# Second LayerNorm of blocks 0 to 3: sums turned in 32x32 blocks on VectorE, rows stored in 128-byte runs

## The chip, the cores and the metric

The kernel runs on one core of one Trainium2 chip. The metric is the device time of one execution in microseconds (us); the median of three runs is given. Of the core's engines, TensorE multiplies matrices and, through a product with the identity, turns them; VectorE and ScalarE work on tiles; GpSimd has small jobs here; SyncE only issues transfers. A transfer is issued by an engine's instruction and done by 16 DMA engines beside it.

## The reference

One layer of a hybrid decoder: a projection, four token mixers, an output projection, then an MLP with squared ReLU, each followed by a LayerNorm on the scaled residual. Only the last line matters here.

```python
def layer_norm(x, g, b):
    xf = x.astype(jnp.float32)
    mu = jnp.mean(xf, -1, keepdims=True)
    var = jnp.mean(jnp.square(xf - mu), -1, keepdims=True)
    return ((xf - mu) * lax.rsqrt(var + LN_EPS) * g + b).astype(x.dtype)
...
x = layer_norm(ALPHA * x + mix, ln1_g[l], ln1_b[l])
x = layer_norm(ALPHA * x + sq_relu_mlp(x, w_ff1[l], w_ff2[l]), ln2_g[l], ln2_b[l])
```

2080 tokens (2048 of a prompt, 32 of eight decoded sequences) of 1024 channels are computed in fp32. The MLP has 4096 hidden channels.

## The kernel before

The tokens are cut into 5 blocks of 416 (BLK). Activations lie channels first: a tile is 128 channels x 416 tokens, 8 tiles (KT) are a block's 1024 channels. Every fp32 product is made of three of rounded values: each weight tile (128 x 1024, 512 KB) and each activation is split into a high part (ScalarE, L1391 for weights) and the rest (VectorE, L1917), and TensorE does high x high, high x low and low x high (L1106 to L1108) for the 8 channel tiles: 24 matmuls of 416 columns.

After the input projections and the first part of the attention the program is one long list of steps n, one weight tile each. A block has 72 steps (STEPS_B); base_of(b) is its first, and r counts from there. Its steps are "up" and "down" tiles of the MLP in turns (0 to 7 up, 8 to 15 down, and so on), then the next block's output projection. Each engine's program walks through the same steps and does at each what is due:

- SyncE, at step n, requests weight tile n + 4 (load_weights, L650). It waits until VectorE has split tile n + 2, since two raw tiles have a place (w_raw). Behind that, in this order, come transfers of an attention unit (load_q L667, load_k L677, load_v L704), the gather of one K page in four transfers (gather_k, L774) and stores of finished rows (store_row, L756). It runs its program strictly in order.
- ScalarE, at step n, finishes the activation of tile n - 1 if that is an up tile (hidden), then splits tile n + 2 (hi_ahead), once step n - 1 is done (three split tiles have a place), then makes the two sigmoids of the attention unit of this step (L1360, L1364).
- VectorE, at step n, adds the result of tile n - 1 or makes the low part of its activation (hidden_lo, L1944), in block 3 does sample work, splits tile n + 2 (lo_ahead), then does its part of the attention, then of a LayerNorm.
- TensorE, at step n, starts with the scores of the step's attention unit (L950, L951). They wait for ScalarE's sigmoids of the unit before, since the scores have a single PSUM bank. In every fourth such step it multiplies the attention output (L965). Then come the 24 matmuls.

Attention units stand in steps 8 to 53, 8 to 59 and 8 to 53 of blocks 0, 1 and 2. The gathers stand in two of three steps until step 47 of block 2. Block 3 has the attention of the decoded sequences instead: from step K_AT = 10 on VectorE turns two K pages (turn_pages, L2154) at each step, ahead of its split of the weights. SyncE loads the first four at step 9 (L524).

The second LayerNorm of block b - 1 is done in steps 1, 2, 4 and 6 of block b (ROWS2), a group of 104 rows at each. TensorE turns the sums (acc, "mlp_sum") of the group into rows, with 8 transposes into two PSUM banks (forward, L1139). VectorE takes mean and variance of each row from there (bn_stats, L1958; bn_aggr), ScalarE the root (L1428), VectorE scales and adds (L2127, L2129) into nat3, and SyncE stores the group one step later. nat3 shares its place with other tiles (pages of the samples, y_block, the first LayerNorm's work tiles), so load_y and the first K pages of block 3 wait for the stores (s_out). Block 4's rows are done after the last step, and this the change leaves alone.

## Time and profile before

| | us |
|---|---|
| median of three runs | 2357.74 (2355.44 to 2365.38) |
| the profiled execution | 2362.01 |
| its span, first to last instruction | 2360.3 |
| TensorE busy with matmuls | 2308.6 |
| VectorE busy | 1534.7 |
| ScalarE busy | 1143.7 |
| GpSimd busy | 211.0 |

TensorE's granted clock was 0.995 of full over the span. Busy time is a union: neighbours that overlap are counted once. In a listing by group the mean is that of one instruction from its start to its end, so that a mean may be above the pace at which such instructions follow each other. The DMA engines were busy 48.7% of their time for SyncE's queue. Splitting a weight tile takes ScalarE 1.05 us and VectorE 1.22, the low part of an activation 0.59. Issuing the store of a row group keeps SyncE for 0.42 us in the median (0.40 to 0.51), and the next request follows 0.55 us after its start (956.27 to 956.82 in block 1).

### The profile page before, as it was taken

Reading aid. Unit: us, or ns where it says so; the run is one execution under the profiler, and the core shown is the slowest. Engines: PE = TensorE matmul, PEld = TensorE weight load, DVE = VectorE, ACT = ScalarE, POOL = GpSimd, SP = SyncE. Lnnn points to the kernel's source line nnn. Section 1 sums busy time; section 2 is a strip of 40 time slices with the busy share of each in tenths; the row PEclk is TensorE's granted clock in tenths of the full one; section 3 lists DMA queues with packets and bytes.
Section 4 is the critical chain, followed back from the end, with each engine's and each line's share of the span. In section 5 each row is a group of like instructions: output and inputs, shape, how many; then the busy total and the mean of one; then the engine's idle time right before and its main releaser. Section 6 shows DMA issues by size and latency. Waiting matters only on the chain.

```text
span 2360.3 us, 45447 instructions
## 1 busy us (share of the span) xinstructions
PE 2308.6 (98%) x17231; PEld 2217.8 (94%) x17231; DVE 1534.7 (65%) x2175; ACT 1143.7 (48%) x1740; POOL 211.0 (9%) x464
## 2 busy tenths in 40 slices
PE   7999999999999999999999999999999999999998
PEld 6999999899989999999999999999988889999997
DVE  7545661845777778777778778767876426854435
ACT  5466522545546545465464555544534425444432
POOL 0012230200111100100110011100000320000000
PEclk9999999999999999999999999999999999999999
DMA  8434553644665544665654556543377774343332
GB/s 260 147 111 141 164 176 133 190 134 126 164 194 171 157 143 132 170 189 145 187 154 135 159 150 189 164 133 126 119 280 239 252 233 146 107 146 116 117 115 83
DMA packets 219180, 377.38 MB, mean 160 GB/s; under 512 B 105409, under 2 KB 140738, under 8 KB 218834
## 3 DMA queue, kind: packets, MB, share of 16 engines
q1 hardware_dynamic: 209682, 346.45, 48.7%
q0 software_dynamic: 9280, 28.02, 3.7%
q8 instruction: 137, 2.24, 0.4%
q14 instruction: 81, 0.66, 0.1%
HBM read 327.37 MB, written 63.80 MB: 166 GB/s over the span
## 4 chain that ended last, share of the span: by engine, by line
PE 91%; DVE 2%; ACT 2%; DMA 2%; issue 1%; SPq 1%; DVEq 0%; ACTq 0%
PE PS L1106 22%; PE PS L1108 22%; PE PS L1107 21%; PE PS L890 5%; PE PS L892 5%; PE PS L891 5%; PE PS L965 3%; PE PS L951 1%; PE PS L950 1%; DMA w_raw<-w_all 1%; PE PS L1030 1%; PE PS L1005 1%; PE PS L930 1%; PE PS L1139 1%; DVE w_hi_lo L1917 1%
## 5 line engine op out<-in xcount | busy, mean ns | idle before, releaser
L1391 ACT ACTIVATE w_hi_lo<-w_raw 128x1024 fp32r<-128x1024 f32 x240 | 252.9, 1054 | 366.7 <-PE PS L1108 292.9
L1106 PE MATMUL PS<-a_hi,w_hi_lo 128*128 128x416 f32 x1080 | 383.3, 355 | 2.8 <-issue 1.6
L1108 PE MATMUL PS<-a_hi,w_hi_lo 128*128 128x416 f32 x1080 | 379.3, 351 | 0.8 <-issue 0.8
L1107 PE MATMUL PS<-a_lo,w_hi_lo 128*128 128x416 f32 x1080 | 378.5, 350 | 0.0
L1917 DVE TENSOR_TENSOR w_hi_lo<-w_raw,w_hi_lo 128x1024 fp32r<-128x1024 f32 x240 | 292.5, 1219 | 79.0 <-ACT w_hi_lo L1391 77.2
L1106 PE MATMUL PS<-h_hi,w_hi_lo 128*128 128x416 f32 x824 | 291.1, 353 | 0.0
L1108 PE MATMUL PS<-h_hi,w_hi_lo 128*128 128x416 f32 x824 | 289.3, 351 | 0.0
L1107 PE MATMUL PS<-h_lo,w_hi_lo 128*128 128x416 f32 x824 | 288.2, 350 | 0.4 <-issue 0.4
L1944 DVE TENSOR_TENSOR h_lo<-h_full,h_hi 128x416 fp32r<-128x416 f32 x160 | 94.5, 591 | 249.2 <-ACT h_hi L1406 249.0
L1106 PEld LDWEIGHTS PS<-a_hi,w_hi_lo 128*128 128x128 f32 x1080 | 203.1, 188 | 11.7 <-issue 7.5
L1402 ACT ACTIVATE h_full<-PS 128x416 f32<-128x416 f32 x160 | 82.3, 514 | 261.4 <-PE PS L1108 255.2
L1107 PEld LDWEIGHTS PS<-a_lo,w_hi_lo 128*128 128x128 f32 x1080 | 203.4, 188 | 4.8 <-issue 1.7
L1391 ACT ACTIVATE w_hi_lo_c<-w_raw 128x1024 fp32r<-128x1024 f32 x120 | 126.4, 1053 | 167.9 <-PE PS L1108 154.9
L1108 PEld LDWEIGHTS PS<-a_hi,w_hi_lo 128*128 128x128 f32 x1080 | 202.7, 188 | 2.3
L1106 PE MATMUL PS<-a_hi,w_hi_lo_c 128*128 128x416 f32 x520 | 185.1, 356 | 3.5 <-DVE a_lo L1950 3.3
L1108 PE MATMUL PS<-a_hi,w_hi_lo_c 128*128 128x416 f32 x520 | 183.9, 354 | 0.0
L1107 PE MATMUL PS<-a_lo,w_hi_lo_c 128*128 128x416 f32 x520 | 183.1, 352 | 0.0
L1872 DVE TENSOR_TENSOR_SCAN n_prompt<-n_prompt 128x512 f32<-128x512 f32 (+3 forms) x160 | 177.4, 1109 | 4.6 <-POOL n_prompt L2389 3.9
L1917 DVE TENSOR_TENSOR w_hi_lo_c<-w_raw,w_hi_lo_c 128x1024 fp32r<-128x1024 f32 x120 | 146.3, 1219 | 38.6 <-ACT w_hi_lo_c L1391 37.4
L1106 PEld LDWEIGHTS PS<-h_hi,w_hi_lo 128*128 128x128 f32 x824 | 154.6, 188 | 7.4 <-issue 4.7
L1107 PEld LDWEIGHTS PS<-h_lo,w_hi_lo 128*128 128x128 f32 x824 | 154.9, 188 | 3.2
L1937 DVE TENSOR_TENSOR mlp_sum<-mlp_sum,PS 128x416 f32<-128x416 f32 x117 | 68.6, 587 | 135.6 <-PE PS L1108 134.4
(313 smaller groups left out, 4708.3 us busy)
## 6 DMA issues: line engine op xcount, KB each, us to landing
...
k_gathered<-ck SPq DMA_DIRECT2D x512, 32.0 KB
...
proj_scratch<-stage SPq DMA_DIRECT2D x70, 208.0 KB, 2.0
...
```

The costliest lines, as they stand in the source:

```text
L890: pe.matmul(out, w_h, x_hi(b)[:, k, :], start=(k == 0), stop=False)
L891: pe.matmul(out, w_h, x_lo(b)[:, k, :], start=False, stop=False)
L892: ins = pe.matmul(out, w_l, x_hi(b)[:, k, :], start=False, stop=(k == KT - 1))
L965: ins = pe.matmul(PS[HD * side:HD * side + HD, 3 + quarter, first * 32:P], vq[rows, k + side, :], wt[rows, v % 2, first:4, k + side, :], s ...
L1106: pe.matmul(out, w_h, mh_[:, k, :], start=(g == 0), stop=False)
L1107: pe.matmul(out, w_h, ml_[:, k, :], start=False, stop=False)
L1108: ins = pe.matmul(out, w_l, mh_[:, k, :], start=False, stop=(g == KT - 1))
L1391: act.activation(halves(w_hi(n)), raw_halves(n), ACT.Copy).then_inc(s_wh, 1)
L1402: act.activation(hf[:, f % 2, :], PS[:, (N_P + n) % 3, 0:BLK], ACT.Relu).then_inc(s_r, 1)
L1872: dve.tensor_tensor_scan(rev(n_t[:, 0:w]), rev(n_t[:, 0:w]), rev(n_t[:, 0:w]), n_t[:, w:w + 1], ALU.mult, ALU.bypass).then_inc(s_scan2, 1)
L1917: dve.tensor_tensor(halves(w_lo(n)), raw_halves(n), halves(w_hi(n)).bitcast(F32), ALU.subtract).then_inc(s_wl, 1)
L1944: dve.tensor_tensor(hl[:, i, :], hf[:, f % 2, :], hh[:, i, :].bitcast(F32), ALU.subtract).then_inc(s_hl, 1)
```

## The change

For blocks 0 to 3 nothing is turned on TensorE any more. VectorE's transpose turns each 32x32 block of a tile for itself. Applied to acc[:, k, :], 128 channels x 416 tokens, it gives a tile in which partition 32 q + j, at place (i, 32 k + c), holds token 32 i + j and channel 128 k + 32 q + c. So each group of 32 partitions, a quadrant, holds for every token a quarter of its channels. Mean and variance of those 256 values are taken, and joined over the four quadrants with two small products with a matrix gmean, which holds 0.25 where partition numbers agree modulo 32: one for the mean, one for the variance within plus the squared deviation of the quadrant's mean. The gains and shifts are loaded a second time in the quadrants' order (gq). A row of the output is then four times eight runs of 32 values, and the store of one channel tile and one quadrant is a transfer of 32 partitions x 13 runs of 128 bytes; a block has 32 of them.

The work is placed in steps 0 to 7 of the next block, the stores in steps 8 and 9 behind everything else that SyncE issues in those steps. The sample attention of block 3 starts two steps later (K_AT = 12, V_AT = 35), and its first K pages are loaded in step 11. TensorE waits at step 8 for the variance instead of the rows.

```diff
-ROWS2 = (1, 2, 4, 6)
+TB = BLK // 32
+PART = ((0, 7), (7, TB))
+SCALED_AT = (6, 7)
+STORED = 16 * 4 * KT
+MEAN_AT = {base_of(b) + r: (b - 1, which) for b in range(1, NB) for which, r in enumerate((4, 5))}
...
-K_AT, V_AT = 10, 33
+K_AT, V_AT = 12, 35
...
-            def store_row(b, j):
-
-                sp.wait_ge(s_row, b * NR + j + 1)
-                sp.dma_start(y_out[b * BLK + j * ROW:b * BLK + (j + 1) * ROW], nat3[0:ROW, j, :]).then_inc(s_out, 16)
+            def store_rows(b, ks):
+
+                rows = y_out[b * BLK:(b + 1) * BLK].rearrange("(i j) (k r c) -> k r j i c", j=32, r=4, c=32)
+                sp.wait_ge(s_row, b + 1)
+                for k in ks:
+                    for q in range(4):
+                        sp.dma_start(rows[k, q], nat4[32 * q:32 * q + 32, :, 32 * k:32 * k + 32]).then_inc(s_out, 16)
...
             sp.dma_start(gb2[:, :, :], rows2).then_inc(s_gb, 16)
+            for q in range(4):
+                rows = rows2[32 * q:32 * q + 32].rearrange("p n (k r c) -> p n k r c", r=4, c=32)[:, :, :, q, :]
+                sp.dma_start(gq[32 * q:32 * q + 32, :, :].rearrange("p n (k c) -> p n k c", c=32), rows).then_inc(s_gb, 16)
...
-                    if r == 9:
-                        sp.wait_ge(s_out, 16 * NR * 3)
+                    if r == 11:
+                        sp.wait_ge(s_out, STORED * 3)
                         for u in range(RING):
                             k_load(sp, u)
...
-                if b >= 1 and r - 1 in ROWS2:
-                    store_row(b - 1, ROWS2.index(r - 1))
+                if b >= 1 and r in (8, 9):
+                    store_rows(b - 1, range(4 * r - 32, 4 * r - 28))
...
-            def norm2_row(b, j):
-
-                if j == 0:
-                    pe.wait_ge(s_fev, (b + 1) * FT)
-                if j >= 2:
-                    pe.wait_ge(s_row, b * NR + j - 1)
-                forward(acc, 0, j, 0)
+            def norm2_stat(b, which):
+
+                if b == 0 and which == 0:
+                    pe.wait_ge(s_gmean, 1)
+                pe.wait_ge(s_qst, 2 * b + which + 1)
+                src = qsq[:, :] if which else qmv[:, :, 0]
+                pe.matmul(PS[:, 4 + which, 0:TB], gmean[:, :], src, start=True, stop=True).then_inc(s_qsum, 1)
...
+            def norm2_turn(b, ks):
+
+                wait_apart(dve, s_fev, (b + 1) * FT)
+                for k in ks:
+                    own.up(dve.transpose(nat4[:, :, 32 * k:32 * k + 32], acc[:, k, :]))
+
+            def norm2_spread(first, last):
+
+                for i in range(first, last):
+                    own.up(dve.bn_stats(qbn[:, i, :], nat4[:, i, :]))
+
+            def norm2_gain(first, last):
+
+                for i in range(first, last):
+                    own.up(dve.scalar_tensor_tensor(out=nat4[:, i, :], in0=nat4[:, i, :], scalar=qmean[:, i:i + 1], in1=gq[:, 0, :],
+                                                    op0=ALU.subtract, op1=ALU.mult))
+
+            def norm2_rows(b, part):
+
+                for i in range(*PART[part]):
+                    ins = dve.scalar_tensor_tensor(out=nat4[:, i, :], in0=nat4[:, i, :], scalar=qrstd[:, i:i + 1], in1=gq[:, 1, :],
+                                                   op0=ALU.mult, op1=ALU.add)
+                if part:
+                    ins.then_inc(s_row, 1)
+                else:
+                    own.up(ins)
+
+            def norm2(b, r):
+
+                if r == 0:
+                    norm2_turn(b, range(4))
+                if r == 1:
+                    norm2_turn(b, range(4, KT))
+                    own.sync()
+                    norm2_spread(0, 4)
+                if r == 2:
+                    norm2_spread(4, TB)
+                    own.sync()
+                    for i in range(TB):
+                        ins = dve.bn_aggr(qmv[:, i, :], qbn[:, i, :])
+                    ins.then_inc(s_qst, 1)
+                if r == 4:
+                    dve.wait_ge(s_qst, 2 * b + 1)
+                    dve.wait_ge(s_qsum, 2 * b + 1)
+                    own.up(dve.tensor_tensor(qdev[:, :], qmv[:, :, 0], PS[:, 4, 0:TB], ALU.subtract))
+                    op(dve.tensor_copy(qmean[:, :], PS[:, 4, 0:TB]))
+                    op(dve.tensor_tensor(qsq[:, :], qdev[:, :], qdev[:, :], ALU.mult))
+                    dve.tensor_tensor(qsq[:, :], qsq[:, :], qmv[:, :, 1], ALU.add).then_inc(s_qst, 1)
+                    if b == 0:
+                        dve.wait_ge(s_gb, 80)
+                    norm2_gain(0, 5)
+                if r == 5:
+                    dve.wait_ge(s_qsum, 2 * b + 2)
+                    dve.tensor_scalar(qstd[:, :], PS[:, 5, 0:TB], EPS, None, ALU.add).then_inc(s_qve, 1)
+                    norm2_gain(5, TB)
+                if r == 6:
+                    dve.wait_ge(s_qsd, b + 1)
+                    op(dve.reciprocal(qrstd[:, :], qstd[:, :]))
+                if r in SCALED_AT:
+                    norm2_rows(b, SCALED_AT.index(r))
```

SyncE in steps 8 to 10 of block 1, from the request of tile 12 on; y_out is the output, "nat" is nat3, "rows_turned" is nat4. Before:

```order
L650 DMA w_raw<-w_all 128x1024 [waits w_lo_made]
L667 DMA q_rows<-proj_scratch 64x512 [waits q_lo_made]
...
L774 DMA k_gathered<-ck 128x1x64
L650 DMA w_raw<-w_all 128x1024 [waits w_lo_made]
L704 DMA v_quarters<-v_scratch 32x1024 [waits av_done,v_tile_stored]
L704 DMA v_quarters<-v_scratch 32x1024 x3
L677 DMA k_rows<-kv_out 64x512 [waits k_lo_made]
L677 DMA k_rows<-kv_out 64x512
L650 DMA w_raw<-w_all 128x1024 [waits w_lo_made]
```

and with the change:

```order
L667 DMA w_raw<-w_all 128x1024 [waits w_lo_made]
L684 DMA q_rows<-proj_scratch 64x512 [waits q_lo_made]
...
L794 DMA k_gathered<-ck 128x1x64
L776 DMA y_out<-rows_turned 32x13x32 [waits row_scaled]
L776 DMA y_out<-rows_turned 32x13x32 x15
L667 DMA w_raw<-w_all 128x1024 [waits w_lo_made]
L721 DMA v_quarters<-v_scratch 32x1024 [waits av_done,v_tile_stored]
L721 DMA v_quarters<-v_scratch 32x1024 x3
L694 DMA k_rows<-kv_out 64x512 [waits k_lo_made]
L694 DMA k_rows<-kv_out 64x512
L776 DMA y_out<-rows_turned 32x13x32 [waits row_scaled]
L776 DMA y_out<-rows_turned 32x13x32 x15
L667 DMA w_raw<-w_all 128x1024 [waits w_lo_made]
```

Sixteen stores now stand between the requests of tiles 12 and 13, and sixteen more between those of tiles 13 and 14.

SyncE in steps 1 to 10 of block 4, where only weights and rows are moved. Before:

```order
L650 DMA w_raw<-w_all 128x1024 [waits w_lo_made] x20
L756 DMA y_out<-nat 104x1024 [waits row_scaled]
L650 DMA w_raw<-w_all 128x1024 [waits w_lo_made]
L756 DMA y_out<-nat 104x1024 [waits row_scaled]
L650 DMA w_raw<-w_all 128x1024 [waits w_lo_made] x2
L756 DMA y_out<-nat 104x1024 [waits row_scaled]
```

and with the change:

```order
L667 DMA w_raw<-w_all 128x1024 [waits w_lo_made] x26
L776 DMA y_out<-rows_turned 32x13x32 [waits row_scaled]
L776 DMA y_out<-rows_turned 32x13x32 x15
L667 DMA w_raw<-w_all 128x1024 [waits w_lo_made]
L776 DMA y_out<-rows_turned 32x13x32 [waits row_scaled]
L776 DMA y_out<-rows_turned 32x13x32 x15
```

The four single stores, a step or two apart, have become two rows of sixteen with one weight request between them.

VectorE in steps 0 to 2 of block 1 with the change; before, each of steps 1, 2, 4 and 6 held two statistics, a join, the small ones and two scalings of 104x1024:

```order
L2126 STREAM_TRANSPOSE rows_turned<-mlp_sum 128x13x32 [waits mlp_evacuated]
L2126 STREAM_TRANSPOSE rows_turned<-mlp_sum 128x13x32 x3
L1953 TENSOR_TENSOR h_lo<-h_full,h_hi 128x416 [waits h_hi_made]
L1928 TENSOR_TENSOR w_hi_lo<-w_raw,w_hi_lo 128x2x512 [waits w_hi_made]
L2126 STREAM_TRANSPOSE rows_turned<-mlp_sum 128x13x32 [waits mlp_evacuated]
L2126 STREAM_TRANSPOSE rows_turned<-mlp_sum 128x13x32 x3
L2131 BN_STATS quadrant_bn<-rows_turned 128x6 [waits dve_own]
L2131 BN_STATS quadrant_bn<-rows_turned 128x6 x3
L1953 TENSOR_TENSOR h_lo<-h_full,h_hi 128x416 [waits h_hi_made]
L1928 TENSOR_TENSOR w_hi_lo<-w_raw,w_hi_lo 128x2x512 [waits w_hi_made]
L2131 BN_STATS quadrant_bn<-rows_turned 128x6 x9
L2161 BN_AGGR quadrant_mean_var<-quadrant_bn 128x2 [waits dve_own]
```

Everything down to the 13 joins stands ahead of TensorE's first small product, which is in the middle of step 4.

## Rows read from the trace of the kernel before

**Rows 1.** The page: busy time of the engines, and the last chain by engine.
```profile
PE 2308.6 (98%) x17231; PEld 2217.8 (94%) x17231; DVE 1534.7 (65%) x2175; ACT 1143.7 (48%) x1740; POOL 211.0 (9%) x464
PE 91%; DVE 2%; ACT 2%; DMA 2%; issue 1%; SPq 1%; DVEq 0%; ACTq 0%
```
**Rows 2.** Waits of TensorE: who waited for whom, us in total, times, longest.
```profile
PE PS L1106 <- DVE a_lo L1950: 3.3, 4, 1.6
```
**Rows 3.** The chain in block 1's step 1: start, length, what.
```profile
915.71 0.87 PE PS L1139 x8
```
**Rows 4.** TensorE's timeline in step 50 of block 3: start, length, engine, line, operation.
```profile
1949.22 0.35 PE L1108 MATMUL PS<-a_hi,w_hi_lo_c 128*128 128x416 f32 x1
1949.41 0.53 PE L1042 MATMUL PS<-row_pairs,y_rows 128*128 128x32 f32 x4
...
1950.05 0.35 PE L1107 MATMUL PS<-a_lo,w_hi_lo_c 128*128 128x416 f32 x1
```
**Rows 5.** VectorE's timeline in block 1, and groups by form (busy, mean ns of one).
```profile
919.68 1.29 DVE L1958 BATCH_NORM_STATS2 bn<-PS 104x6 f32<-104x512 f32 x2
...
924.66 0.58 DVE L1944 TENSOR_TENSOR h_lo<-h_full,h_hi 128x416 fp32r<-128x416 f32 x1
...
L1887 DVE STREAM_TRANSPOSE w_turned<-s_prompt 128x384 f32<-128x384 f32 x16 | 9.1, 572 | 0.0
...
L2035 DVE SCALAR_TENSOR_TENSOR nat<-nat,rstd,gb 104x512 f32<-104x512 f32 x8 | 5.6, 747 | 0.2
```
**Rows 6.** SyncE: two lines' instructions, a timeline row, and the page's transfers with landings.
```profile
L695 SPq DMA_DIRECT2D v_scratch<-v_made x32: 594/628/1286, 414.0 to 1209.4; - x32
...
L764 SPq DMA_DIRECT2D q_sample<-proj_scratch x4: 427/428/432, 1680.1 to 1682.9; - x4
...
1207.34 2.66 SPq L695 DMA_DIRECT2D v_scratch<-v_made  x4
...
v_scratch<-v_made SPq DMA_DIRECT2D x32, 64.0 KB, 3.4
...
proj_scratch<-stage SPq DMA_DIRECT2D x70, 208.0 KB, 2.0
```
**Rows 7.** SyncE's timeline in steps 8 to 10 of block 1.
```profile
960.66 3.22 SPq L774 DMA_DIRECT2D k_gathered<-ck  x4
963.93 0.47 SPq L650 DMA_DIRECT2D w_raw<-w_all  x1
...
967.54 0.58 SPq L650 DMA_DIRECT2D w_raw<-w_all  x1
```
**Rows 8.** ScalarE's timeline in block 1; TensorE's scores at step 13 of blocks 1 and 2.
```profile
968.46 1.06 ACT L1391 ACTIVATE w_hi_lo<-w_raw 128x1024 fp32r<-128x1024 f32 x1 [3.26 <-DMA w_raw<-w_all]
...
970.56 0.63 ACT L1342 ACTIVATE q_hi_lo<-q_rows 128x512 fp32r<-128x512 f32 x1
...
979.98 0.39 PE L950 MATMUL PS<-k_hi_lo,q_hi_lo 128*128 128x512 f32 x1
...
1368.65 0.39 PE L950 MATMUL PS<-k_hi_lo,q_hi_lo 128*128 128x512 f32 x1
```
**Rows 9.** SyncE's timeline in block 2, then in block 3 with VectorE's two page turns.
```profile
1350.93 0.48 SPq L650 DMA_DIRECT2D w_raw<-w_all  x1
...
1721.26 0.33 SPq L650 DMA_DIRECT2D w_raw<-w_all  x1
1724.82 1.75 SPq L524 DMA_DIRECT2D pages<-k_gathered  x4
...
1728.93 2.50 DVE L2154 STREAM_TRANSPOSE k_pages_turned<-pages 128x1024 f32<-128x1024 f32 x2 [1.30 <-DMA pages<-k_gathered]
```
**Rows 10.** Block 4: a tile request of SyncE, ScalarE's splits at steps 10 and 11.
```profile
2093.01 45.64 SPq L650 DMA_DIRECT2D w_raw<-w_all  x11
...
2098.03 1.06 ACT L1391 ACTIVATE w_hi_lo<-w_raw 128x1024 fp32r<-128x1024 f32 x1 [3.03 <-PE PS L1108]
2102.56 1.06 ACT L1391 ACTIVATE w_hi_lo<-w_raw 128x1024 fp32r<-128x1024 f32 x1 [3.47 <-PE PS L1108]
```

More of the change, by code:

```diff
@@ L838, in _ @@
                         load_x1(b + 1)
-                    if r == (40 if b < 3 else 50):
+                    if r == (40 if b < 3 else 51):
                         load_y(b + 1)
@@ L1097, in dense @@
                         norm1_stat(*STAT_AT[n])
+                    if n in MEAN_AT and g == 4:
+                        norm2_stat(*MEAN_AT[n])
                     if i == 0:
@@ L2009, in last_rows @@
             def last_rows(js, between):
-                e = NR * NB
+                e = NR
                 two = slice(js[0], js[1] + 1)
@@ L2116, in norm1_back, with quadrant_mean @@
                     dve.tensor_tensor(al[:, k, :], xr[:, k, :], ah[:, k, :].bitcast(F32), ALU.subtract).then_inc(s_xl, 1)
-            def norm2_row(b, j):
-                e = NR * (b + 1) + j
-                row_var(e)
-                row_rstd(e)
-                bank = 4 + 2 * (j % 2)
-                row = nat3[0:ROW, j, :]
-                if b == 0 and j == 0:
-                    dve.wait_ge(s_gb, 16)
-                op(dve.scalar_tensor_tensor(out=row, in0=PS[0:ROW, bank:bank + 2, :].rearrange("p a b -> p (a b)"),
-                                            scalar=mv[0:ROW, j, 0:1], in1=gb2[0:ROW, 0, :], op0=ALU.subtract, op1=ALU.mult))
-                dve.scalar_tensor_tensor(out=row, in0=row, scalar=rstd[0:ROW, j:j + 1], in1=gb2[0:ROW, 1, :], op0=ALU.mult,
-                                         op1=ALU.add).then_inc(s_row, 1)
+            def quadrant_mean():
+                m = gmean[:, 0:32]
+                op(dve.tensor_tensor(m, ident[:, 0:32], ident[:, 32:64], ALU.add))
+                for q in (2, 3):
+                    op(dve.tensor_tensor(m, m, ident[:, 32 * q:32 * q + 32], ALU.add))
+                op(dve.tensor_scalar(m, m, 0.25, None, ALU.mult))
+                for q in (1, 2, 3):
+                    own.up(dve.tensor_copy(gmean[:, 32 * q:32 * q + 32], m))
+                own.sync()
+                dve.sem_inc(s_gmean, 1)
```

71 lines of the change are left out of this document (31 added, 40 removed).

## Prediction

> **What bounds the kernel now.** I read the page's busy times and its chain first: TensorE is busy for 98% of the span, and 91% of the chain that ended last is its matmuls [rows 1]. Next come TensorE's waits: behind the input projections the largest is 3.3 us in all [rows 2]. So TensorE's instruction stream sets the time, an instruction taken out of it pays in full, and another engine costs nothing until TensorE waits for it. The question is therefore how much each edit removes from that stream, and which other engine comes near enough to hold it up.
>
> A weight tile costs 24 matmuls, one step of 4.53 us where nothing else is in it; rows on ScalarE 4.53 us apart show that [rows 10]. In steps with an attention unit it is 5 us, and about 7.2 where the attention output is multiplied too. I call step r the r-th of a block and count blocks from 0. SyncE runs through the same steps; in step r it requests the tile of step r + 4 as soon as VectorE has split that of r + 2. ScalarE splits tile r + 4 in step r + 2. A late request thus has up to two steps before ScalarE wants it and two more before TensorE does. In blocks 1 and 2 the second pair doesn't count: ScalarE makes the sigmoids of an attention unit behind its split of the weights, and TensorE's next scores wait for them.
>
> **Taken from TensorE.** The second LayerNorm of a block turned its four row groups with 8 transposes each, 128 in four blocks; on the chain one group is 0.87 us [rows 3]. 16 x 0.87 = 13.9 us go. All of it is on the bounding engine.
>
> **Added to TensorE.** Two fp32 products per block, 128x13. The nearest rows are two fp32 products with 32 columns: they put 0.83 us between the matmul before them and the second behind them, where 0.38 is usual [rows 4]. That is 0.45 for two, 1.8 us for four blocks. Cost of PE edits: -13.9 + 1.8 = -12.1 us.
>
> **VectorE.** Before, a row group took from 919.68 to 924.66, 5.0 us, four times a block [rows 5]. Now come 8 transposes of 416 columns at about 0.60 (384 columns take 0.57), 13 statistics of 256 values at somewhat over half the 0.65 of 512, say 0.36, 13 joins of them at an estimated 0.2, and 26 scalings of 256 values at half the 0.75 of 512 values plus 0.1 [rows 5]: 4.8 + 4.7 + 2.6 + 12.4 and 1 us of small ones, 25.5 against 20 us. It is spread over steps 0 to 7, where 8 x 1.65 us of other work (the lower halves of weights and activations) leave 23 of 36 us; what doesn't fit runs some 2 us into step 8, before the stores of the rows can start anyway. So it is hidden. The nearest call is TensorE's first product in the middle of step 4: it wants the 13 joined statistics. From 919.68 on, where its first statistics stand now, VectorE has 2.4 + 1.4 + 1.65 + 3.2 + 2.6 = 11.3 us to do and ends at 931.0; TensorE would come to it at about 915.7 + 3.5 x 4.53 = 931.6 [rows 3, 5]. Hidden by a hair; if statistics of 256 cost the full 0.65 each, it is late by 3 to 4 us in each block. I take 0, and 0 to 16 us for the range. ScalarE's four roots become one: off the path.
>
> **SyncE's queue: the term that decides.** A block's rows were stored in 4 requests of 0.42 us, one in steps 2, 3, 5 and 7. Now they take 32 requests, 16 in step 8 and 16 in step 9, each 32 partitions x 13 runs of 128 bytes. The queue's own instructions take time on SyncE. The nearest row is the store of the turned V tile: 32 partitions x 16 runs of 128 bytes, median 0.63 us, and four of them in 2.66 [rows 6]. I take 0.66 each: 10.6 us for 16, in steps of 4.5 to 5 us. The request for tile 13 stands behind 16 of them, that for tile 14 behind 32. The lower bound for one is the 0.47 at which requests with 2 such runs follow each other, the upper the 0.80 of the page gathers (4 in 3.22) [rows 6, 7]. The data keeps up with that as far as a row tells: such a store lands after 3.4 us, 1.4 more than one with long runs [rows 6].
>
> Block by block, in the clock of the trace of before (removed transposes shift everything alike):
> - Block 1. Tile 13 was requested at 963.93 and ScalarE started on it at 968.46, tile 14 at 967.54 [rows 7, 8]. 0.55 us of the old store goes, 10.6 comes: tile 13 at 974.0. 3.6 us of V and K requests follow, then 10.6 more: tile 14 at 988.2. It lands 4.5 later (as tile 13 did), 992.7, and the sigmoids behind its split are done 2.1 later, 994.8 (968.46 to 970.56 in the rows). TensorE's scores of step 13 stood at 979.98 [rows 8]. **14.8 us lost.**
> - Block 2, with the same steps. 1350.93 - 0.55 + 10.6 = 1361.0; + 3.6 + 10.6 = 1375.2; + 4.5 + 2.1 = 1381.8 against 1368.65 [rows 8, 9]. **13.1 us.**
> - Block 3 has no attention and no gathers, but SyncE waits in step 11 for all stores of block 2 before it loads K pages into their place, and VectorE turns two pages before it splits tile 14. Tile 12 is requested at 1721.26; the last store is issued at 1742.7 and lands 3.4 later, 1746.0; pages take 4.1 (1724.82 to 1728.93), two turns 2.5 and the split 1.2: 1753.8. TensorE ends step 8 some 0.5 us behind the request of tile 12 (in block 4: 2098.03 - 4.53 against 2093.01), at 1721.8, and would start tile 14 five steps and some 0.9 us of sample work later, at 1745.3 [rows 9, 10]. **8.5 us.**
> - Block 4. Tile 12 at 2093.0, tile 14 at 2114.9, landed 4.5 later, split on both engines after 2.3 more: 2121.7. TensorE ends step 9 at 2098.0 and wants the tile at 2098.0 + 4 x 4.53 = 2116.1 [rows 10]. **5.6 us.**
>
> Together 42.0 us. Afterwards SyncE catches up, since what it has to issue in other steps takes less than a step. The four loads of the rearranged gains, 2.6 us, stand once ahead of the trunk's first tile requests, inside the two steps of lead that a tile has: nothing.
>
> **Sum.** -12.1 + 42.0 = +29.9 us. On the profiled execution, 2362.0, that is 2391.9; it lies 4.3 above the median of 2357.7, so I predict **2387.5 us** as a median, +1.3%.
>
> The Trainium skill, DMA: Bandwidth & Descriptors, section "Anatomy of one DMA", calls descriptor generation small and says that many descriptors can be emitted before their cost shows. By that rule a request with 416 runs costs SyncE no more than one for a weight tile; the first rival below is what this would make of the time. The trace disagrees where it can be compared, 0.63 us with 512 runs against 0.33 for a weight tile [rows 6, 9], though the shapes differ in more than their runs.
>
> **Rivals.**
> 1. Requests are cheap. At 0.37 each (a weight tile's 0.33 [rows 9] and a gap of 0.04) 16 take 5.9 us, so each block is 9.4 better: losses of 5.4, 3.7, 0 and 0, sum -3.0, 2355 us. At 0.47 it is 6.2 better: 8.6 + 6.9 + 2.3 + 0 = 17.8, sum +5.7, 2363 us. Against it: the row with 16 runs; for it: that 64 short runs took only 0.43. Chance 0.16.
> 2. Nothing waits: the stores hide entirely behind the lead of four tiles and only TensorE's saving is seen, 2346 us, faster by 0.5%. It decides at about 4 us for 16 requests, below any row. Against it is also that ScalarE already waited 3.26 us for tile 13 in block 1 [rows 8]. Chance 0.08.
> 3. The 128-byte writes are slow in the queues, so that weights behind them are late too. If each held its queue for the 1.14 us that the longer landing allows (1.4 x 416 / 512), 16 take 18.2 us, 15.2 more per block: +90.7 us, 2448 us. Against it: the landing of 3.4 us was measured on stores of which four were issued in 2.66, so they can't have held the queues for long. Chance 0.08. The same page, section "Specifications", sets 512 bytes as the least for full rate and says that shorter writes are read, modified and written; the 1.4 us is all that this trace shows of it.
> 4. The mechanism of the forecast with VectorE's statistics at their dear end, or with the gathers' 0.80 for a store (+4.5 per block): 2403 to 2406. I count this in the forecast's case.
>
> **How the numbers follow.** The forecast's case, SyncE late in all four blocks, has 0.68 and spans 2375 to 2410. The range holds it and most of the cheap requests: **2358 to 2412**. A measurement here tells 0.5%, 12 us, from no change. Faster by more: rival 2 at its edge and a share of rival 1, 0.08. Within: 0.16. Slower: 0.76.
>
> **What would show it.** TensorE: 8 products of 128x13 in place of 128 transposes. SyncE: 16 stores in a row, about 10.6 us, twice a block, and the tile requests behind them 10 and 20 us later than now. TensorE idle, in blocks 1 and 2 at the scores of step 12 or 13 and released by ScalarE, in blocks 3 and 4 at tile 14 and released by VectorE's split; 5 to 15 us at each block, none elsewhere. ScalarE's waits for w_raw grow to tens of us. I am wrong if 16 stores take 6 us or less, if the idle time sits at the products of steps 4 and 5 (then it was VectorE), or if stores are on time and weights still land late (rival 3).

## The result

| | before | after |
|---|---|---|
| median, us | 2357.55 (4 runs) | 2383.18 (4 runs) |
| the profiled execution, us | 2362.01 | 2378.09 |
| its span, us | 2360.3 | 2376.5 |
| TensorE busy, us | 2308.6 | 2305.7 |
| granted clock over the span | 0.995 | 0.993 |

The change makes the kernel slower: the ratio is 1.0085, with a 95% interval of 1.0062 to 1.0109, some 20 us. One of the four runs of after was disturbed (2540 us, at a clock of 0.846) and is not in the ratio; the other three lie between 2378.09 and 2385.53, with a median of 2380.83. I had predicted 2387.5, 29.9 us above the kernel before.

The page of the profile after, in the parts that [rows 1] shows of before:

```profile
PE 2305.7 (97%) x17119; PEld 2212.5 (93%) x17119; DVE 1547.7 (65%) x2334; ACT 1145.3 (48%) x1728; POOL 209.0 (9%) x464
PE 81%; SPq 6%; DVE 5%; DMA 3%; ACT 3%; issue 2%; POOLq 0%; ACTq 0%; DVEq 0%; POOL 0%
```

TensorE has 112 instructions fewer (128 transposes went, and the 8 products stand in the trace as two records each), yet it holds 81% of the chain where it held 91%, and SyncE's queue 6% where it held 1%. TensorE's busy time fell by only 2.9 us although 14 us of transposes went; the rest of this document shows why.

TensorE's waits (who waited for whom: us in total, times, longest), which answer to the single row of [rows 2]:

```profile
PE PS L973 <- ACT n_prompt L1380: 17.3, 8, 4.0
...
PE PS L1131 <- DVE w_hi_lo_c L1928: 6.4, 3, 4.7
...
PE PS L1053 <- DMA pages<-cv: 1.8, 1, 1.8
```

L973 is the first product of the scores (L950 of before), waiting for ScalarE's sigmoids, and L1131 the first matmul of a weight tile, waiting for VectorE's split: the two places that were forecast. Of the first kind before had

```profile
PE PS L950 <- ACT n_prompt L1364: 3.3, 3, 1.8
```

and neither of the other two was among its longest waits. How it comes about in block 1 is seen first on SyncE (start, length, engine, line, what), to be held against [rows 7]:

```profile
958.99 8.23 SPq L776 DMA_DIRECT2D y_out<-rows_turned  x16
967.27 0.47 SPq L667 DMA_DIRECT2D w_raw<-w_all  x1
...
971.09 9.56 SPq L776 DMA_DIRECT2D y_out<-rows_turned  x16
980.70 0.47 SPq L667 DMA_DIRECT2D w_raw<-w_all  x1
```

then on ScalarE, which answers to [rows 8]:

```profile
971.53 1.06 ACT L1407 ACTIVATE w_hi_lo<-w_raw 128x1024 fp32r<-128x1024 f32 x1 [9.49 <-DMA w_raw<-w_all]
...
984.29 1.06 ACT L1407 ACTIVATE w_hi_lo_c<-w_raw 128x1024 fp32r<-128x1024 f32 x1 [10.03 <-DMA w_raw<-w_all]
...
985.82 0.68 ACT L1380 ACTIVATE n_prompt<-PS,nbias_h 128x512 f32<-128x512 f32 x1
```

and on TensorE:

```profile
973.79 0.79 PE L973 MATMUL PS<-k_hi_lo,q_hi_lo 128*128 128x512 f32 x1 [4.00 <-ACT n_prompt L1380]
...
986.55 0.50 PE L973 MATMUL PS<-k_hi_lo,q_hi_lo 128*128 128x512 f32 x1 [3.66 <-ACT n_prompt L1380]
...
987.96 0.55 PE L1131 MATMUL PS<-h_hi,w_hi_lo 128*128 128x416 f32 x1
988.30 0.55 PE L1132 MATMUL PS<-h_lo,w_hi_lo 128*128 128x416 f32 x1
...
991.13 0.35 PE L1132 MATMUL PS<-h_lo,w_hi_lo 128*128 128x416 f32 x1
991.32 0.35 PE L1133 MATMUL PS<-h_hi,w_hi_lo 128*128 128x416 f32 x1
```

Tile 13 is requested at 967.27 behind sixteen stores, tile 14 at 980.70 behind sixteen more. ScalarE idles 9.49 and 10.03 us for them, its sigmoids stand behind the split, and TensorE's scores stand behind the sigmoids. What I had not reckoned with is in the last four rows: behind a wait the matmuls follow each other at 0.34 us, and three microseconds later at 0.19 again. The page's windows (stretch; its length, TensorE's busy time and matmuls; granted clock; DMA share; GB/s) show the reason:

```profile
960.00:970.00 10.00, 9.79 (x52) 1.00 0.66 125
970.00:980.00 10.00, 6.00 (x140) 0.83 0.83 166
980.00:990.00 10.00, 6.34 (x27) 0.87 0.51 141
990.00:1000.00 10.00, 10.00 (x54) 0.96 0.78 196
```

In before all four read 10.00 busy at a clock of 1.00. The clock was granted at half (1.2 GHz in place of 2.4) for a stretch of 3.4 us at or just behind the end of each of the two waits, from 973.70 and from 987.35. At 0.34 for 0.19 that is ten matmuls where eighteen would have gone, 1.5 to 1.7 us each time. In the slow stretches TensorE counts as busy, so this loss stands in no list of waits.

The trace of before has the same thing twice behind shorter waits, one in block 0 (2.88 us, at 806.3) and one in block 1:

```profile
1224.97 0.46 PE L1106 MATMUL PS<-a_hi,w_hi_lo_c 128*128 128x416 f32 x1 [1.57 <-DVE a_lo L1950]
...
1227.49 0.79 PE L950 MATMUL PS<-k_hi_lo,q_hi_lo 128*128 128x512 f32 x1 [1.11 <-ACT n_prompt L1364]
```

with this window around it:

```profile
1220.00:1230.00 10.00, 7.32 (x31) 0.86 0.50 168
```

**A ledger.** ScalarE reads each up tile's result as soon as TensorE has it. There are 160 such readings in every kernel, so the start of each, less its start in before, tells how far a kernel is ahead or behind there. In us, + is behind; each column is what a stretch added, by block and steps ("1: 7-16" is block 1, from the reading of step 7 to that of step 16), the last one the whole span:

| kernel | 1: 7-16 | 1: 16-32 | 2: 7-16 | 3: 7-16 | 4: 7-16 | span |
|---|---|---|---|---|---|---|
| after | 11.4 | 1.5 | 9.3 | 4.2 | 1.8 | 2376.5 |
| e1 one store | 0.1 | 2.6 | -0.5 | -2.1 | 0.0 | 2342.4 |
| e2 short runs | 8.3 | 2.0 | 6.8 | 3.1 | 0.0 | 2367.1 |
| e3 long runs | 7.7 | 7.1 | 6.7 | 3.8 | 0.0 | 2376.3 |
| e4 spread | 2.8 | 6.2 | 3.8 | 5.9 | 0.0 | 2367.7 |
| e5 gathers aside | 0.0 | 1.9 | -0.5 | 5.0 | 0.0 | 2347.1 |
| e6 two queues | 0.0 | 5.4 | -0.5 | -1.9 | 0.0 | 2347.7 |
| e7 ScalarE's queue | 0.1 | 1.8 | -0.4 | 1.2 | 0.0 | 2351.3 |
| e8 rows, no gathers | 7.9 | 7.9 | 7.9 | 5.5 | 3.8 | 2378.3 |
| e9 halves | 0.0 | 0.0 | -0.5 | -1.5 | 0.0 | 2341.3 |
| e10 old, plus rows | 9.3 | -0.4 | 5.9 | 0.0 | 0.3 | 2370.0 |

Spans differ in a few us beyond this, from waits and half-clock stretches at places that have nothing to do with the change (before has 4.8 us of them at 806): e1 was already 5 us ahead of before, and after level with it, when block 1 began. Comparisons between kernels go by the ratios of the timed runs and by the columns, not by the spans.

### The profile page after: what moved, and what is told of

Read it like the earlier page. It is cut to its first block, busy times and chain, and to the rows that moved or that the text cites. A ratio compares the mean times of both kernels' runs of the same rounds, so it can differ in the third digit from the quotient of the medians.

```text
span 2376.5 us, 45460 instructions
## 1 busy us (share of the span) xinstructions
PE 2305.7 (97%) x17119; PEld 2212.5 (93%) x17119; DVE 1547.7 (65%) x2334; ACT 1145.3 (48%) x1728; POOL 209.0 (9%) x464
## 4 chain that ended last, share of the span: by engine, by line
PE 81%; SPq 6%; DVE 5%; DMA 3%; ACT 3%; issue 2%; POOLq 0%; ACTq 0%; DVEq 0%; POOL 0%
PE PS L1131 19%; PE PS L1133 19%; PE PS L1132 19%; PE PS L913 5%; PE PS L915 5%; PE PS L914 5%; SPq L776 3%; PE PS L988 3%; DMA w_raw<-w_all 2%; DVE w_hi_lo L1928 1%; SPq L794 1%; PE PS L973 1%; PE PS L974 1%; ACT w_hi_lo L1407 1%; DVE rows_turned L2142 1%
## 5 line engine op out<-in xcount | busy, mean ns | idle before, releaser
L1131 PE MATMUL PS<-a_hi,w_hi_lo 128*128 128x416 f32 x1080 | 382.1, 354 | 1.3 <-DVE w_hi_lo L1928 1.3
L1131 PE MATMUL PS<-h_hi,w_hi_lo 128*128 128x416 f32 x824 | 292.3, 355 | 0.0
L1131 PEld LDWEIGHTS PS<-a_hi,w_hi_lo 128*128 128x128 f32 x1080 | 202.7, 188 | 10.5 <-issue 6.2
L1131 PE MATMUL PS<-a_hi,w_hi_lo_c 128*128 128x416 f32 x520 | 184.3, 354 | 3.5 <-DVE a_lo L1959 3.4
L1131 PEld LDWEIGHTS PS<-h_hi,w_hi_lo 128*128 128x128 f32 x824 | 155.6, 189 | 8.2 <-issue 5.3
L1131 PE MATMUL PS<-h_hi,w_hi_lo_c 128*128 128x416 f32 x432 | 154.1, 357 | 8.5 <-DVE w_hi_lo_c L1928 6.3
```

Of the source, the lines that this page charges most:

```text
L1131: pe.matmul(out, w_h, mh_[:, k, :], start=(g == 0), stop=False)
```

## The experiments

**Without the rows of stores.** e1 keeps one store a block, and all of the change on TensorE and VectorE.

```diff
-                    for q in range(4):
-                        sp.dma_start(rows[k, q], nat4[32 * q:32 * q + 32, :, 32 * k:32 * k + 32]).then_inc(s_out, 16)
+                    if k == 0:
+                        sp.dma_start(rows[k, 0], nat4[0:32, :, 0:32]).then_inc(s_out, 16)
```

> The changed kernel with one store a block in place of 32 (the other 31 are left out, so rows of blocks 0 to 3 are missing from the output); TensorE's and VectorE's part of the change stays as it is. Theory (SyncE's rows of 16 requests make TensorE late): no idle time at the scores of blocks 1 and 2 nor at the tiles of blocks 3 and 4, no stretch at half clock behind it, only TensorE's saving of about 12 us is left: 2346 us, ratio to the kernel before 0.995. Rival (the longer work of VectorE, or the two small products, cost TensorE something that I had at nothing): the time stays above 2355 us and idle time is seen in steps 4 to 8 of blocks 1 to 4.

Measured: 2348.86 us, ratio 0.9956 (0.9938 to 0.9973). The page's busy times:

```profile
PE 2295.7 (98%) x17119; PEld 2205.9 (94%) x17119; DVE 1547.4 (66%) x2334; ACT 1143.7 (49%) x1728; POOL 215.2 (9%) x464
```

TensorE is 12.9 us less busy than before and the losses in steps 7 to 16 are gone. VectorE works as long as in after (1547 us) and holds nobody up. The cost of the change is in the 31 other stores of each block; whether in their requests or in what they write, the next experiments show.

**What a request costs SyncE.** e2 keeps the 32 requests but cuts each from 13 runs a partition to one; e3 keeps requests and bytes, but makes each partition's part one run.

```diff
-                        sp.dma_start(rows[k, q], nat4[32 * q:32 * q + 32, :, 32 * k:32 * k + 32]).then_inc(s_out, 16)
+                        sp.dma_start(rows[k, q][:, 0:1], nat4[32 * q:32 * q + 32, 0:1, 32 * k:32 * k + 32]).then_inc(s_out, 16)
```

> The changed kernel with all 32 store requests of a block, but each writes one run of 128 bytes for each of its 32 partitions, where there were 13 (most of the rows of blocks 0 to 3 are left out of the output). Theory A (SyncE pays for the runs that a request is cut into): a request takes about 0.35 us as one for a weight tile does, 16 take 5.6 us, almost no tile is late, about 2350 us. Theory B (SyncE pays for the request, whatever it holds): 16 still take 8.2 to 9.8 us and the time stays at 2375 to 2380 us. With B the bytes in the queues have no part in it either.

```diff
+                flat = y_out[b * BLK:(b + 1) * BLK].rearrange("t c -> (t c)").rearrange("(m p f) -> m p f", m=4 * KT, f=BLK)
...
-                        sp.dma_start(rows[k, q], nat4[32 * q:32 * q + 32, :, 32 * k:32 * k + 32]).then_inc(s_out, 16)
+                        src = nat4[32 * q:32 * q + 32, :, :].rearrange("p i c -> p (i c)")[:, BLK * k:BLK * (k + 1)]
+                        sp.dma_start(flat[4 * k + q], src).then_inc(s_out, 16)
```

> The changed kernel with 32 requests of the same bytes (32 partitions x 1664 bytes), each partition's in one run in place of 13 of 128 bytes; the rows of blocks 0 to 3 are written in another order than the output's. Theory A (SyncE pays for runs): 0.35 us a request, about 2350 us. Theory B (SyncE pays for the request): 8.2 to 9.8 us for 16, 2375 to 2380 us. If this one is fast and the one with short requests too, it is the number of runs; if only the one with fewer bytes is fast, it is the traffic.

Measured: e2 2368.69 us, ratio 1.0044 (1.0029 to 1.0060); e3 2373.74 us, 1.0053 (1.0037 to 1.0070). SyncE's rows of sixteen in block 1, of e2:

```profile
955.03 7.44 SPq L776 DMA_DIRECT2D y_out<-rows_turned  x16
...
966.30 8.77 SPq L776 DMA_DIRECT2D y_out<-rows_turned  x16
```

and of e3:

```profile
958.81 7.43 SPq L777 DMA_DIRECT2D y_out<-rows_turned  x16
...
970.08 8.26 SPq L777 DMA_DIRECT2D y_out<-rows_turned  x16
```

Theory B is near, though both times lie under the 2375 to 2380 us that it gave. Sixteen requests take 7.4 to 8.8 us with 32 runs each and 8.2 to 9.6 with 416: nine tenths of the cost belongs to the request, one tenth to its runs. A thirteenth of the bytes (e2) and all of them (e3) cost SyncE about the same (63.5 and 63.0 us for all eight rows of sixteen, against 70.6 in after), so the bytes have no part in it. The lower time against after comes from that tenth: in block 1 the two rows are 1.6 us shorter together, and one half-clock stretch is gone with it, which makes the 3.1 us between 11.4 and 8.3. That e3 loses 5 us more than e2 in steps 16 to 32 is another matter, to which e9 comes.

**The row alone, in the old kernel.** e10 is the kernel before with nothing of the change but rows of sixteen requests.

```diff
+                if b in AGAIN and r in (8, 9):
+                    if r == 8:
+                        sp.wait_ge(s_out, out_of(b - 1) + 64)
+                    for m in range(16):
+                        j, q = divmod(m, 4)
+                        at, c0 = 26 * q, BLK * (r - 8)
+                        first = (b - 1) * BLK + j * ROW + at
+                        sp.dma_start(y_out[first:first + 26, c0:c0 + BLK], nat3[at:at + 26, j, c0:c0 + BLK]).then_inc(s_out, 16)
...
```

> The kernel before, with its transposes on TensorE, its four stores a block and its VectorE work, and nothing of the change but requests on SyncE: sixteen more in step 8 and sixteen in step 9 of blocks 1, 2 and 4 (block 3 has none, since K pages take the place there), each storing 26 partitions x 1664 bytes of rows that are stored already. Theory (a row of sixteen requests is enough to make TensorE late, whatever came with it): blocks 1, 2 and 4 lose about what they lost with the change and long runs, 7.7, 6.2 and 0.2 us, up to its 11.7, 9.3 and 1.8: 2374 to 2382 us, ratio 1.006 to 1.0095. Rival (the losses need the change's later statistics on VectorE as well): under 1.003.

Measured: 2375.91 us, ratio 1.0073 (1.0051 to 1.0095). SyncE's two rows in block 1,

```profile
957.40 6.73 SPq L851 DMA_DIRECT2D y_out<-nat  x16
...
967.92 7.79 SPq L851 DMA_DIRECT2D y_out<-nat  x16
```

and TensorE's wait there:

```profile
PE PS L966 <- ACT n_prompt L1380: 6.1, 3, 4.8
```

9.3, 5.9 and 0.3 us are lost in blocks 1, 2 and 4, at the same place and by the same releaser. A row of sixteen requests, with its writes, is enough. With e1, the change without the rows, both directions are shown.

**Spreading the stores.** e4 issues four stores in each of steps 8 to 15; block 3 is left as it is.

```diff
-                if b >= 1 and r in (8, 9):
+                if b == 3 and r in (8, 9):
                     store_rows(b - 1, range(4 * r - 32, 4 * r - 28))
+                if b in (1, 2, 4) and 8 <= r < 16:
+                    store_rows(b - 1, (r - 8,))
```

> The changed kernel, complete, with the 32 stores of a block issued four in each of the steps 8 to 15 in blocks 1, 2 and 4; in block 3 they stay sixteen in each of steps 8 and 9, since K pages wait for them. Theory (only their standing in a row hurts): four requests take about 2.3 us of a step of 4.5 to 7 us, the idle time and the half-clock stretches of blocks 1, 2 and 4 go (11.7, 9.3 and 1.8 us lost there between step 7 and step 16 in the profile), those of block 3 stay: about 2355 us as an execution, ratio about 0.999. Rival (SyncE has no room left for 18 us of requests next to gathers and attention loads, or the writes of 128 bytes slow the weights in the queues wherever they stand): the losses move to steps 10 to 16 and the time stays above 2368 us.

Measured: 2369.33 us, ratio 1.0045 (1.0029 to 1.0061). The rival's time. Block 4, where SyncE only has weights to request, loses nothing any more. Blocks 1 and 2 still lose 9.0 and about 8 us, only later. The chain of waits of e4 from 970 to 1040, by line,

```profile
by line: DMA w_raw<-w_all 25.2%; SPq L794 21.0%; SPq L776 12.5%; issue 8.0%; SPq L721 6.2%; SPq L791 6.1%; DVE w_hi_lo L1930 5.3%; ACT w_hi_lo L1409 4.6%; SPq L667 4.5%; SPq L694 3.3%; SPq L684 1.6%; SPq L739 0.8%; DVE s_prompt L1892 0.7%; 
```

and the pieces of one step (start, length, what):

```profile
970.90 0.47 SPq L667
971.41 0.47 SPq L791
972.33 0.70 SPq L794
...
975.56 0.48 SPq L776
...
977.63 0.56 SPq L667
```

TensorE's matmuls are not in the chain at all: for 70 us SyncE, and the weights that it requests late, set the time. A gather is not the 3.2 us of its four requests but 4.2, since the load of the page's number (L791) and what follows it stand ahead. Between the tile requests at 957.89 and 1004.63, eight steps and 46.7 us, SyncE has 8 tile requests of 0.5, 5 gathers of 4.2, two sets of V and K loads of 3.0 and seven groups of stores of 2.1: 45.7 us. Without the stores it would be 31.0. SyncE had a third of its time free there, and the stores take nearly all of it, whether they stand in a row or not.

**Room for them, and other queues.** e5 adds to e4 that gathers skip the steps 8 to 15 of blocks 1 and 2 and are made up later. e6 adds to e5 that in block 3 ScalarE issues half of the stores. e7 is the change with all stores on ScalarE's queue and the gathers where they were. e8 is the change with its two rows and only the gathers moved.

```diff
-GATHER_AT = {PRE + 1 + (3 * n) // 2: n for n in range(PGN)}
+GATHER_STEPS = [n for n in (PRE + 1 + (3 * m) // 2 for m in range(2 * PGN))
+                if not ((n - PRE) // STEPS_B in (1, 2) and 8 <= (n - PRE) % STEPS_B < 16)]
+GATHER_AT = {GATHER_STEPS[n]: n for n in range(PGN)}
```

> The kernel with stores four a step in steps 8 to 15 (blocks 1, 2, 4), and the page gathers of the same steps in blocks 1 and 2 taken out of them and made up at the end of their row, so that they end some 16 steps later in block 2; complete. With the stores spread alone, blocks 1 and 2 still lost 7.6 and 7.1 us, in steps 9 to 30, and the chain of waits ran through SyncE there: a gather keeps it for 4.2 us with the page number's load ahead of it, and stands in two of three steps. Theory (SyncE has no room for gathers and stores together): without gathers in these eight steps the losses of blocks 1 and 2 go, block 3's 6 us stay, ratio to the kernel before 0.998 to 0.999. Rival (writes in 128-byte runs slow the weights in the queues): blocks 1 and 2 still lose 7 us each, ratio 1.0045 as before.

```diff
+                if b == 3 and r in (8, 9, 10):
+                    store_rows(sp, b - 1, *((0, 6), (6, 12), (12, 16))[r - 8])
...
+                    if b == 3 and r in (8, 9, 10):
+                        store_rows(act, b - 1, *((16, 22), (22, 28), (28, 32))[r - 8])
```

> The same, and in block 3 ScalarE issues half of the 32 stores: six, six and four in steps 8, 9, 10 on each of the two queues; complete. Theory: SyncE is back in time for tile 14 (3.3 us of requests a step in place of 9), so block 3's 4 to 6 us go as well, and all that is left is TensorE's 12 us and what the later sample attention gives: ratio 0.995 to 0.996, as with one store a block. Rival (the late start of block 3's K pages, which need all 32 stores landed, is what costs, or ScalarE's six requests make its splits late): block 3 keeps 3 us or more.

```diff
-                if b >= 1 and r in (8, 9):
-                    store_rows(b - 1, range(4 * r - 32, 4 * r - 28))
...
+                    if b == 3 and r in (8, 9, 10):
+                        store_rows(act, b - 1, *((0, 11), (11, 22), (22, 32))[r - 8])
+                    if b in (1, 2, 4) and 8 <= r < 16:
+                        store_rows(act, b - 1, 4 * (r - 8), 4 * (r - 7))
```

> All 32 stores of a block issued by ScalarE, four a step in steps 8 to 15 (11, 11 and 10 in steps 8 to 10 of block 3), gathers where the change has them; complete. The same transfers at about the same time as with the stores spread over SyncE, from another engine's queue. Theory (SyncE's time is what is short): blocks 1 and 2 lose nothing on SyncE, though ScalarE pays 2 us a step behind its sigmoids, which it has since it is busy for under half its time: ratio 0.996 to 0.999. Rival A (traffic): 1.0045 as with SyncE. Rival B (ScalarE's own order: requests ahead of its splits make tiles late): idle time of TensorE in steps 9 to 16, released by ScalarE.

e8's only edit is that of the gathers above.

> The changed kernel with its two rows of sixteen stores as they are, and only the gathers of steps 8 to 15 of blocks 1 and 2 moved behind; complete. Theory: the requests of tiles 13 and 14 come one gather (4.2 us) earlier and SyncE catches up sooner, so of the 11.7 and 9.3 us of blocks 1 and 2 about 4 go in each, with the half-clock stretches that go with them up to 7: time 2368 us, ratio 1.003 to 1.006. If gathers had no part in it, it stays at 1.0085.

Measured: e5 2356.09 us, ratio 0.9985 (0.9963 to 1.0007); e6 2350.04, 0.9959 (0.9943 to 0.9976); e7 2352.72, 0.9972 (0.9954 to 0.9990); e8 2381.10, 1.0083 (1.0050 to 1.0116).

e5: blocks 1 and 2 lose nothing in steps 7 to 16, with the same writes in the same steps as in e4. Block 3 keeps its 5.0 us, one wait:

```profile
PE PS L1135 <- DVE w_hi_lo_c L1932: 5.1, 1, 5.1
```

e6: this wait is gone as well. e7 leaves the gathers and the rest of SyncE's program alone and has the writes of e4 in the steps of e4, and blocks 1 and 2 lose 0.1 us and nothing in steps 7 to 16. In e5 the same writes go through SyncE's own queue and cost nothing there either. So the writes in 128-byte runs slow TensorE by nothing that these runs show; SyncE's time was what was short. In blocks 1 and 2 ScalarE pays less than I gave it. Its queue (ACTq) and its activations in a step of block 1:

```profile
955.04 1.06 ACT L1406 ACTIVATE w_hi_lo<-w_raw 128x1024 fp32r<-128x1024 f32 x1 [2.78 <-PE PS L1132]
955.59 0.91 ACTq L592 DMA_DIRECT2D y_out<-rows_turned  x2
956.00 0.67 ACT L1375 ACTIVATE s_prompt<-PS,bias_h 128x512 f32<-128x512 f32 x1
```

Requests are issued while an activation runs, and the split still waits for TensorE. In block 3, with 11, 11 and 10 requests in three steps, it is otherwise:

```profile
1719.09 7.28 ACTq L592 DMA_DIRECT2D y_out<-rows_turned  x10
1726.41 0.37 ACT L1529 ACTIVATE v_new<-PS 32x256 f32<-32x256 f32 x1 [6.29 <-issue]
```

The next split stands behind these ten, and TensorE waited 1.1 and 1.4 us for weights there. That is rival B of e7 at a small size, with VectorE's split of the late tile as the releaser: block 3 comes to 1.2 in e7 where e1 and e6, with one store and with 16 on ScalarE, have -2.1 and -1.9.

e8 is a miss. In block 1 it gains 3.5 us on after, as the one gather less would give, but in block 2 only 1.4. It then loses 7.9 in steps 16 to 32 of block 1, and in blocks 3 and 4, which the edit doesn't touch, 1.3 and 2.0 more than after. TensorE's idle time in steps 7 to 16 was 5.5 and 5.4 us in blocks 1 and 2 against 7.9 and 6.2; but the granted clock was at half for 6.8 us in each, as in after. Its rows of stores also took longer in block 2 (9.31 and 9.86 us against 8.24 and 9.75) and in block 4 (9.29 and 8.58 against 8.78 and 8.48); why is open. Moving the gathers alone is worth nothing that the timed runs can see.

**The last piece.** In e6, 3.9 us of idle time and a half-clock stretch stood at about step 21 of block 1, and in e3 and e8 more of the same. ScalarE waits there for a weight tile that stands behind the load of the first residual, 1.7 MB in one request. In e6, SyncE's request of that load and of the tile behind it,

```profile
1020.18 0.48 SPq L759 DMA_DIRECT2D x_residual<-x_scratch  x1
1020.71 0.57 SPq L677 DMA_DIRECT2D w_raw<-w_all  x1
```

and ScalarE's split of that tile:

```profile
1032.57 1.06 ACT L1412 ACTIVATE w_hi_lo<-w_raw 128x1024 fp32r<-128x1024 f32 x1 [4.75 <-DMA w_raw<-w_all]
```

e9 cuts the load in two.

```diff
...
                     if r == (20 if b < 3 else 28):
-                        load_x1(b + 1)
+                        load_x1(b + 1, slice(0, 4))
+                    if r == (23 if b < 3 else 31):
+                        load_x1(b + 1, slice(4, KT))
...
```

> The kernel with the stores spread, the gathers aside and two queues in block 3, and in addition the 1.7 MB load of the first residual (step 20 of blocks 0 to 2, step 28 of block 3) cut into two halves three steps apart; complete. In the kernel without this cut block 1 still lost 5.4 us between steps 16 and 32: weights behind this load came late, TensorE waited 3.9 us and fell to half clock once. Theory: behind a load of half the size the weights land 2.5 us earlier, so 4 to 5 us of it go: ratio to the kernel before 0.993 to 0.995. Rival (the gathers, which keep SyncE in its place, and not the size of the load): the loss stays, 0.996.

Measured: 2348.81 us, ratio 0.9951 (0.9936 to 0.9966). The window of e6,

```profile
1020.00:1040.00 20.00, 15.46 (x189) 0.91 0.83 229
```

and of e9:

```profile
1020.00:1040.00 20.00, 19.32 (x218) 1.00 0.77 192
```

The stretch's 5.4 us are gone in the trace. In the timed runs e9 can't be told from e6 (0.9951 and 0.9959, with intervals that overlap almost wholly): e6's 5.4 us may have been a matter of one execution, since e5, with the same code in blocks 1 and 2, lost 1.9 there. Both e6 and e9 are complete kernels and beat the kernel before, by 0.4 to 0.5%, and the changed one by 1.3%.

## Why the prediction came out as it did

**TensorE's own part (-12.1): right.** In e1, steps 0 to 7 of blocks 1 to 4 gain 3.2, 4.6, 3.2 and 3.2 us, counted from the last reading of the block before (step 55), against the forecast 3.0 each; the 4.6 has a half-clock stretch of before in it, at 1227, that e1 doesn't have. A product with 13 columns costs less than taken: the next matmul follows the one before it after 0.32 us in place of 0.19 (935.97 to 936.29), 0.13 for a product against 0.22.

```profile
935.97 0.35 PE L1133 MATMUL PS<-a_hi,w_hi_lo_c 128*128 128x416 f32 x1
936.16 0.29 PE L1203 MATMUL PS<-quadrant_square,quadrant_mean 128*128 128x13 f32 x2
936.29 0.43 PE L1131 MATMUL PS<-a_hi,w_hi_lo_c 128*128 128x416 f32 x1
```

**VectorE (0): right.** By groups (busy, mean ns of one; 52 are 13 in each of four blocks):

```profile
L2142 DVE SCALAR_TENSOR_TENSOR rows_turned<-rows_turned,row_rstd,gb_quadrants 128x256 f32<-128x256 f32 x52 | 21.3, 480 | 0.4
...
L2131 DVE BATCH_NORM_STATS2 quadrant_bn<-rows_turned 128x6 f32<-128x256 f32 x52 | 17.8, 416 | 0.4
L2126 DVE STREAM_TRANSPOSE rows_turned<-mlp_sum 128x416 f32<-128x416 f32 x32 | 16.7, 579 | 0.0
```

The other 52 scalings (L2136) took 21.2 us. With 4.0 us of joins that is 81.0 in all, 20.3 a block where I had 24.5 for the same four items: scalings 0.41 in place of 0.47, joins 0.08 in place of 0.2. The joins ended at 928.9; in the clock of before I had said 931.0. No wait stands at L1203 and e1 confirms it.

**SyncE's price of a request (0.66): too high.** Sixteen took 8.2 to 9.8 us, 0.51 to 0.61 each. Over the two rows that is 3.4 us less than the forecast 21.2 in block 1 and 3.2, 3.6 and 3.9 in the others. The bounds (0.47 and 0.80) held it. I took the V tile's store as the nearest row because of its short runs, and e2 and e3 show that runs make a tenth of the cost. What set 0.66 against 0.33 for a weight tile is then something other than the number of runs; I can't say what, since e3's requests differ from a weight tile's in partitions and place of the destination too. The Trainium skill (DMA: Bandwidth & Descriptors, section "Anatomy of one DMA — SWDGE (gpsimd) path") says of transfers that GpSimd issues that many descriptors can be emitted before their cost shows; I had applied it to SyncE, of which that section doesn't speak. For SyncE these runs point the same way, 0.05 us between 416 runs and 32, so I was also wrong to read the 0.63 us of 512 runs as evidence against it. What I missed in it is that it says nothing of the half microsecond that the request takes by itself.

**The losses (42.0): the mis-sized term.** The places, the order and the releasers were right in all four blocks; steps 7 to 16 lost 11.4, 9.3, 4.2 and 1.8, together 26.7. TensorE's idle time in it is 7.9, 6.2, 4.7 and 1.6 us, 20.4 in all, half of what I had put. By term:

- Block 1, forecast 14.8 at the scores of step 13. The request of tile 14 stood at 980.70; before's clock with the 3.1 us by which after was then ahead makes that 983.8, against 988.2. 3.4 of it is the rows' pace. The landing took 3.6 in place of 4.5. That leaves 9.5, and the scores at 986.55 were late by 9.7 in the same clock (979.98). Their wait is 7.9 us (4.00 + 0.2 + 3.66) and a first half-clock stretch; the second, behind it, adds 1.7: 11.4.
- Block 2, forecast 13.1, by the same terms: rows 3.2 us quicker, the scores at 1380.22 late by 7.7 (after was then 3.8 behind), and a second half-clock stretch: 9.3.
- Block 3, forecast 8.5: rows 2.7 us sooner by the end of the last, and the stores had landed 1.4 us behind the last request, not 3.4. SyncE behind its last store (which ended at 1749.32), then VectorE, then TensorE:

```profile
1750.68 1.77 SPq L541 DMA_DIRECT2D pages<-k_gathered  x4
```
```profile
1755.40 1.25 DVE L2205 STREAM_TRANSPOSE k_pages_turned<-pages 128x1024 f32<-128x1024 f32 x1 [8.54 <-DMA pages<-k_gathered]
```
```profile
1759.22 0.71 PE L1131 MATMUL PS<-h_hi,w_hi_lo_c 128*128 128x416 f32 x1 [4.69 <-DVE w_hi_lo_c L1928]
```

  The order is the forecast one: stores landed, pages, two turns, split. TensorE wanted the tile at 1754.5, which is 1745.2 in the clock of before; I had said 1745.3. It waited 4.7, and a half-clock stretch added 1.7; sample work that now comes two steps later gave 2.1 in this stretch, as e1's -2.1 shows.
- Block 4, forecast 5.6: rows 3.9 sooner, 1.7 left, 1.8 measured.

**What the sum lacked.** First the clock: five half-clock stretches stand at the waits of blocks 1 to 3, 1.5 to 1.7 us each, some 8 us that partly made good for the losses that were put too high. That the total came as near as some +20 against +29.9 is in this part luck: with the waits sized right and no term for the clock it would have been some +8. The trace of before could have told me: it has two such stretches, behind waits of 2.88 us and of 1.57 and 1.11. Second, 1.8 us in block 3, a wait for V pages that GpSimd gathers, shown among the waits above. Before doesn't have it, e1 does, so it comes with the later V_AT and not with the stores. I had taken the two steps' shift of the sample attention for free. Of the 16.2 us between the spans, steps 0 to 7 of the four blocks gave -14.0 (with the half-clock stretch of before in block 2), the losses +26.7, and all else +3.5.

**"Afterwards SyncE catches up": right of this kernel, and short of a reason.** After lost only 1.4 us in steps 16 to 32. But I had priced a gather at its requests, 3.2 us, and never set SyncE's whole load against the steps. With 4.2 for a gather it is 31 us of 46.7 before the stores are added. Had I made that sum, e4's result could have been told.

**The chances.** Rival 1, cheap requests, came nearest of the others: at 0.47 it gave 2363, and 0.51 to 0.61 lies between it and the forecast's 0.66. Rival 2 didn't come, though e1 shows its time (forecast 2346, measured 2348.9). Rival 3, slow writes, is excluded by e5 and e7. The range (2358 to 2412) held the time with room on both sides.

## What to carry to other kernels

An engine that only issues transfers has a budget as a busy one has: write down what its requests take in a step, register loads among them, and hold that against the step's length before adding to it. The store requests of these kernels cost SyncE 0.41 to 0.61 us each, with 26 to 416 runs and 4 to 53 KB in them, so a layout that turns 4 stores (2.2 us) into 32 (17.3 to 18 us) costs that engine 15 us in a block, and it pays to spread them over steps and queues whose engines have time. A wait on the bounding engine costs more than its length where the clock falls with it.

## What the runs showed of the chip

- Requests in a row on SyncE: 0.41 to 0.49 us each with 26 runs, 0.46 to 0.55 with 32, 0.51 to 0.61 with 416. The second row of sixteen was slower in blocks 1 to 3 (9.56, 9.75 and 9.15 us) than the first (8.23, 8.24 and 8.40). Why is open; in block 4, with only a tile request between them, it was not (8.48 against 8.78).
- Every wait of TensorE of 3.0 to 5.9 us in blocks 1 to 4 of these traces has a stretch of 3.4 or 6.8 us at half clock with it (after, e2 to e6, e8 and e10), and shorter ones can have it too: 2.84 and 2.71 us in block 2 of after, 1.47 in block 2 of e2. A wait of 1.4 us (at about step 21 of block 1 in after) left it at full. Two waits of 1.6 to 1.9 and of 1.1 us at about step 57 of block 1 stand in before, in after and in e1 to e9 alike; the clock fell with them in before, e2, e3, e5, e6, e7 and e9 and stayed at full in after, e1, e4 and e8. So the length of a wait alone doesn't tell.
- ScalarE's requests run beside its activations: four in each step of e7 left its splits where TensorE puts them. Ten in a row took 7.28 us and held the next activation back by 6.29.
